# Repacing the precompute and the sample group of a hybrid decoder layer, and loading the x blocks in order

## The reference, cut to what matters

```python
def token_mix(xn, s0, buf, pos0, p):
    proj = xn @ p['w_in']            # q, k, v, gz, og, u, ga, gb
    ...
    o, s_new = gla_chunked(q, k, v, log_a, s0)
    o = rmsnorm(o, p['gla_norm_g']).reshape(B, T, GLA_VAL_W) * jax.nn.silu(og)
    branch_a = o @ p['w_branch_a']
    pooled, buf_new = pool_mix(u, buf, pos0, p['w_pool_mix'], p['pool_scale'])
    branch_b = pooled @ p['w_branch_b']
    merged = jax.nn.sigmoid(ga) * branch_a + jax.nn.sigmoid(gb) * branch_b
    return merged @ p['w_out'], s_new, buf_new

def decoder_layer(x, mk, mv, s0, buf, pos0, p):
    mix, s_new, buf_new = token_mix(rmsnorm(x, p['norm_mix_g']), s0, buf, pos0, p)
    h = x + mix
    h = h + cross_attn(rmsnorm(h, p['norm_x_g']), mk, mv, p['w_xq'], p['w_xo'])
    h = h + sq_relu_mlp(rmsnorm(h, p['norm_mlp_g']), p['w_up'], p['w_down'])
    return h, s_new, buf_new
```

## Time and profile before

| | us |
|---|---|
| runs of the kernel before | 1319.77, 1319.95, 1322.6 |
| their median | 1319.95 |
| the profiled execution: time / span of its slowest core | 1323.51 / 1321.9 |
| spans of its eight cores | 1307.9 to 1321.9 |
| TensorE (PE) busy | 1263.9 (96%) |
| VectorE (DVE), ScalarE (ACT) busy | 654.9, 650.3 |
| DMA: POOL's queue, SP's queue (share of 16 engines) | 47.2%, 12.0% |

### The profile page before, as it was taken

One profiled execution on the slowest core, in us unless ns is written; L12 is line 12 of the kernel. 1 busy time (PEld: TensorE's weight loads), 2 busy tenths in 40 slices (PEclk: granted clock), 3 DMA queues, 4 the chain that ended last, 5 costly groups with the idle time before them and its releaser, 6 DMA issues.

```text
span 1321.9 us, 23085 instructions; the slowest of 8 cores (1307.9 to 1321.9 us)
## 1 busy us (share of the span) xinstructions
PE 1263.9 (96%) x8426; PEld 643.9 (49%) x8426; DVE 654.9 (50%) x1088; ACT 650.3 (49%) x1333; POOL 67.8 (5%) x131
## 2 busy tenths in 40 slices
PE   3998989999989999999999999999999999999997
PEld 3443645545545554444454445654445554454453
DVE  3463566434546664433576537633244654434446
ACT  2552866756658663111425458764458753120304
POOL 1010000000000000000000001000000000000000
PEclk6898989999999999999999999999999999999999
DMA  9679887327797964566778749435561313333513
GB/s 202 116 129 180 139 148 159 101 75 192 192 265 187 158 115 84 108 113 130 151 147 189 149 74 178 86 66 105 95 184 32 65 32 65 64 68 61 96 33 136
DMA packets 33674, 160.91 MB, mean 122 GB/s; under 512 B 4598, under 2 KB 5246, under 8 KB 22156
## 3 DMA queue, kind: packets, MB, share of 16 engines
q0 software_dynamic: 18112, 104.29, 47.2%
q1 hardware_dynamic: 15452, 55.15, 12.0%
HBM read 241.63 MB, written 22.80 MB: 200 GB/s over the span
## 4 chain that ended last, share of the span: by engine, by line
PE 87%; DMA 8%; issue 1%; DVE 1%; ACT 1%; SPq 0%; DVEq 0%; POOL 0%; ACTq 0%; POOLq 0%
PE pb L805 78%; PE pb L816 5%; PE pb L836 3%; DMA xst_94<-xp 2%; DMA wt_43<-wu 2%; DMA s0f_117<-sgla 2%; DMA kv_150<-ckT 2%; DMA wt_46<-wu 1%; PE pb L826 1%; SPq L909 0%; ACT tmp_95 L855 0%; ACT xn_101 L855 0%; DVE xh L876 0%; DVE xn_102 L876 0%; ACT tmp_99 L855 0%
## 5 line engine op out<-in xcount | busy, mean ns | idle before, releaser
L805 PE MATMUL pb<-actT,wt_45 128*128 128x512 bf16 x704 | 158.6, 379 | 0.6 <-ACT tmp_98 L855 0.5
L876 DVE SCALAR_TENSOR_TENSOR xh<-pb,r_179,xh 128x512 f32<-128x512 f32 x128 | 95.4, 750 | 90.0 <-PE pb L805 88.6
L805 PEld LDWEIGHTS pb<-actT,wt_45 128*128 128x128 bf16 x704 | 68.2, 98 | 81.4 <-issue 1.9
L805 PE MATMUL pb<-actT,wt_46 128*128 128x512 bf16 x448 | 101.3, 379 | 3.2 <-DMA wt_46<-wu 1.9
L805 PE MATMUL pb<-actT,wt_43 128*128 128x512 bf16 x384 | 86.1, 379 | 0.0
L855 ACT ACTIVATE tmp_95<-pb 128x512 f32<-128x512 f32 (+1 forms) x47 | 27.3, 582 | 109.6 <-PE pb L805 97.7
L805 PE MATMUL pb<-wt_44,actT 128*128 128x512 bf16 x320 | 73.1, 379 | 1.6 <-DVE att_109 L865 1.1
L805 PEld LDWEIGHTS pb<-actT,wt_46 128*128 128x128 bf16 x448 | 43.0, 98 | 53.9 <-issue 4.8
L855 ACT ACTIVATE tmp_98<-pb 128x512 f32<-128x512 f32 (+1 forms) x48 | 28.4, 592 | 83.0 <-PE pb L805 80.8
L865 DVE TENSOR_TENSOR xh<-pb,xh 128x512 f32<-128x512 f32 x64 | 44.0, 690 | 48.8 <-PE pb L805 48.5
L805 PE MATMUL pb<-WqK,actT 128*128 128x512 bf16 x256 | 58.5, 379 | 0.0
(11 more groups left out here) (554 smaller groups left out, 2318.5 us busy)
## 6 DMA issues: line engine op xcount, KB each, us to landing
wt_46<-wu POOLq DMA_DIRECT2D x23, 1024.0 KB, 11.2
wt_43<-wu POOLq DMA_DIRECT2D x20, 1024.0 KB, 11.5
wt_44<-wu POOLq DMA_DIRECT2D x20, 1024.0 KB, 10.2
wt_45<-wu POOLq DMA_DIRECT2D x19, 1024.0 KB, 10.5
xh<-xp SPq DMA_DIRECT2D x16, 512.0 KB
yp<-xh SPq DMA_DIRECT2D x15, 512.0 KB, 15.5
wt_43<-wscratch SPq DMA_DIRECT2D x2, 1024.0 KB
s0f_118<-sgla SPq DMA_DIRECT2D x4, 512.0 KB, 5.7
```

What stands on the lines that cost most here:

```text
L805: ins = e.matmul(out, l, r, start=(start and i == 0), stop=(stop and i == m - 1))
L876: return self.g.op(eng, lambda e: e.scalar_tensor_tensor(out=out, in0=in0, scalar=scalar, in1=in1, op0=op0, op1=op1), reads=rd, writes=[ou ...
```

## The change

- In `program`, the loads of blocks 2 to 7 all wait for block 1's load, not block 2's alone.
- In `precompute`, fifteen of the twenty `yield` become `idle(2)`: every step from the memory's normalization on is followed by one that does nothing.
- G is no longer made ahead of the pooling: `tick` makes it in tile 0 at the first tick that finds "pre" at its end, and takes its first step there.
- The C stage has one tick a step, not two (12, not 24, in either tile).
- In `chain`, each of a0, a1, o0, o1, xq0, xq1 takes four steps, not three; each load of keys or values two, not three. An assertion states that the chain has come to the softmax's end in tile 0.

No operation is added or taken away; order, slots and times of issue change.

```diff
@@ program
-            xl.append(d("sp", self.xst[s][:, :], I["xp"][s * 128:(s + 1) * 128, :], after=xl[1:2] if s == 2 else ()))
+            xl.append(d("sp", self.xst[s][:, :], I["xp"][s * 128:(s + 1) * 128, :], after=xl[1:2] if s >= 2 else ()))
@@ tick
     def tick(self):
+        if self.ti == 0 and "G" not in self.gen and self.gen.get("pre", 0) is None:
+            self.gen["G"] = self.sample()
         self.step("G")
@@ tile, ahead of the pooling
         if first:
             self.hook("pool")
-            self.gen["G"] = self.sample()
@@ tile, C stage
             for f, lag in ((M_, 4), (X_, 3), (PT_, 2), (C_, 0)):
                 if 0 <= t - lag < 8 and not (f is M_ and t - lag == 7):
                     f(t - lag)
-            self.tick()
             self.tick()
@@ precompute: after the memory's norm, xk0, xk1, KT, each half of xqT0 and xqT1, xv0, xv1, VT, each half of xo0 and xo1
-        yield
+        yield from self.idle(2)
@@ chain: after a0, a1, o0, o1, xq0, xq1
-            yield from self.idle(3)
+            yield from self.idle(4)
@@ chain, after the softmax
         yield
+        assert self.ti == 0
         while self.ti == 0:
             yield
```

## The result

The changed kernel takes 1330.7 us (median of four runs, 1329.2 to 1332.8). Its ratio to the kernel before is **1.0076 [1.0053, 1.0099]**: slower by some 10 us, where 8 us faster was forecast. The profiled execution has its slowest core at 1329.7 us, against 1321.9 before.

The account below looks back on a forecast made before the run. TensorE bounds the kernel, busy 1263.9 of 1321.9 us. Terms -12 - 7 - 6.6 + 1 + 13.4 + 2 + 1.5 = -7.7 give 1315.8; less 3.6 above the median, forecast 1312 (1304 to 1319; with rivals 1296 to 1325).

Parts of the forecast that it names:

- the packing: Sample's cached key and value loads: two ticks times four meets the buffers' rate; packing costs 1.5 us (0 to 8).
- the precompute: Repaced precompute: gains 7 us at xk1 and 6.6 at xv1, less a cost of 1 for a0's weight.
- The x order: Start of the kernel: with x blocks issued in order, v0's groups run as blocks come; gain 12 us (8 to 15).
- up1: At up1, its weight waits for a1's matmul, run right before it; TensorE idles a whole load; cost 13.4 us (0 to 27).
- the states: State loads on the SP queue in O: five were there and five will be; zero, -3 to +4 us.
- I leave 2 of its 9.0 us: Second xk weight, issued with og0's weight at the same congested place: 2 of its 9.0 us loss remain, gain 7.
- the xv1 stall: Second xv weight in the precompute: its loss of 6.6 us goes as it moves to chunk 5; gain 6.6 (3 to 6.6).
- a0's load: As ga0 begins, a0's weight takes the last xo1 piece's slot: 10.5 us load against up to five gate groups; cost 1.
- seven v0 groups move ahead: At the start, seven v0 groups of 1.73 us (12.1) move ahead of 36.71 us, under the x blocks' arrival.
- the first rival: up1 is not exposed: a1's matmul slips into a spot where TensorE waits in C, hiding the load; 1298 us, chance 0.20.
- The slower rival: up2 is exposed too: o1's matmul runs right before up2 and the same 13.4 us comes again; 1325, chance 0.13.
- The third: Rival at the start: the order of x brings nothing, Part 1 (the x loads) is worth 0; 1324 us, chance 0.12.

Follow-up runs that it names:

- e9: The changed kernel with the precompute's dense pace (one yield a step) and three steps for each load of cached values put back; 1310.5 us.
- e3: The changed kernel with three steps, not two, put back for each load of cached values; 1317.7 us.
- e6: The kernel before with two steps, not three, for each load of cached values; 1323.2 us, ratio 1.0011.
- e5: The changed kernel with the precompute's dense pace put back, sample group still starting at the same late tick; 1321.8 us.
- e1: The kernel before with only the x order changed: loads of blocks 2 to 7 all wait for block 1; 1315.2 us.
- e8: The kernel before with the x order changed and the identF and xsF loads held until block 2 has landed; 1313.7 us.
- e10: The changed kernel with three steps, not four, after each of a0, a1, o0, o1, xq0, xq1; 1349.4 us.
- e4: The changed kernel with two ticks in a step of C and three steps for each load of cached keys and values; 1340.7 us.

## Why the prediction was wrong, point by point

**The sum.** Forecast 1312, measured 1330.7. Two terms carry the miss: the packing came out 11.5 us dearer and the precompute 21.5. The x order adds some 5.5; up1 (13.4) and the states (4.2) erred the other way. Together that is about 21, of 18.7 missed. Taking both terms out (e9) gives 1310.5. That this is near 1312 is luck: by the prediction's own terms e9 would have taken about 1323 (1312, with the precompute's gain of 12.6 taken back and the packing's 1.5 spared).

**Packing of the loads: 1.5 (0 to 8) forecast, 13.0 measured for the values alone** (e3 against after). The step that failed is "two ticks times four is about 28 us, so the rate is met". The rate is met; e6 shows that packing costs nothing measurable in the kernel before. I looked only at the kv ring and not at who else uses the DMA engines when a load comes 6 us earlier: the output stores, which the chain's softmax, moved into dn3 by the late start, had bunched. The interaction of two edits was in none of my terms or rivals. By the ledger 9.3 of 13.7 us are that stall with the lower clock behind it; the other 4.4 are waits that e6 has too, and there wins back.

**The precompute: -13.6 + 1 forecast, about +9 measured** (after against e5). Three steps failed. First, "I leave 2 of its 9.0 us": xk1 and og0's weight still go out within 0.52 us, and now og0's comes second, after 23.8 us; the wait is 6.73 us instead of 6.14. The repacing changed which of the two is late, not that two loads share the stretch. Second, the xv1 stall did go, but small waits for VectorE between 149 and 174 us, the longest 1.08, take 3.6 of its 6.6 us back; and with the dense pace that stall is only 2.50 us, with some time at the lower clock, on e5's core 2. Third, a0's load, priced at 1 (0 to 3), costs 4.3 on core 5 (2.93 idle, the rest lower clock), 3.9 to 4.7 on the other three late cores, and nothing on core 1:

```profile
280.06 2.29 PE L805 MATMUL pb<-o2T,wt_46 128*128 128x512 bf16 x5 [2.93 <-ACT s0b_139 L855]
```

The releaser named is a state's copy; a0's load, issued at 267.18, landed only 0.2 us ahead. Of the ledger's 6.8 us from 80 to 300 (core 5 of after against core 2 of e5), a0's load is 4.3, the stall near 118 us 2.7 (8.9 against 6.2), an idle spot in the pooling 1.1, and the stretch of xv1 gives 1.3 back. Where the other 2 of the 8.9 us lie, the runs don't settle.

**The x order: 12 (8 to 15) forecast, 5.6 to 7.4 measured** (e1), 8.1 in the trace. The mechanism held: v0 runs ahead of the last blocks. Block 7 arrived as taken (by 32.27, forecast 33). The failed step is "seven v0 groups move ahead": by then only two had run. v0's evictions now stand among the blocks' norms on ScalarE, so each waits for the other, and block 2 is taken at 26.77. Holding identF and xsF back (e8) moved block 2 by 5.7 us, block 7 by 1.9 and v1's end by 1.5.

**up1: 13.4 (0 to 27) forecast, 0 measured.** a1's matmul did not run right before up1, but 10 us ahead of it, in a spot where C waited (0.55 us for actT just behind it), as the first rival had it:

```profile
474.04 1.10 PE L816 MATMUL pb<-o2s,wt_46 128*128 128x64 bf16 x32
...
484.47 13.97 PE L805 MATMUL pb<-actT,wt_46 128*128 128x512 bf16 x64
500.47 2.79 PE L805 MATMUL pb<-actT,wt_44 128*128 128x512 bf16 x8 [2.03 <-DMA wt_44<-wu]
```

up1 starts without a wait, but with no slack: its weight landed 0.13 us ahead. On no core did it wait over 0.20. up2's weight costs 2.03 and some lower clock. That such a gap can open, e10 shows, with 4.97 us.

**The states: 0 (-3 to +4) forecast.** Their stretch (300 to 430) loses 4.2 us less than before. They did not leave O: three run among O's matmuls before, four after. What went is the wait for a state: before, each of the eight cores has one there of 2.9 to 5.4 us (the earlier trace rows shows core 7's), after none has. It can come back: core 7 of e9 waits 4.79 us for a state behind O.

**The rivals.** Rival one's mechanism was right, with the time on the other side of its 1298. The slower rival named up2, which shows 2 us, not 13.4. The third, that the order of x brings nothing, is refuted by e1. The range ended at 1325, 6 us short.

## What to carry to other kernels

A transfer's price is not its rate but its company: before a load is moved, list every transfer, stores too, that is in flight in its new place, and who waits for each. Repacing a consumer does not separate two weight loads if both are released by the same event; look at the two issue times first. Where one core of each pair runs late, price each stall for that core, since it sets the time.

## What the runs showed that I had not expected

The same load takes longer on the later core of a pair. a0's weight, first on core 4, then on core 5 of after (KB, us to landing):

```profile
wt_46<-wu POOLq DMA_DIRECT2D x1, 1024.0 KB, 8.9
...
wt_46<-wu POOLq DMA_DIRECT2D x1, 1024.0 KB, 12.6
```

The cores of a pair end 9.3 us apart on average in the kernel before, 20.4 in after and 20.7 in e5, the two with the stall at vt, and 10.8 in e3 and 10.6 in e9, which lack it; but 18.6 in e4 too, whose losses lie elsewhere. The pairs are real: in the 45 runs of before no pair ends closer than 6.3 us, and paired otherwise (0 with 2, 1 with 3, and so on) the cores are only 5.9 apart on average. The Trainium skill, HBM Reference, "Specifications (TRN2)", says that the two cores of a domain share its bandwidth. The rows fit that, but no run here ran one core of a pair alone, so the cause is argued, not shown.
